# Unnormalised probabilities, gates scaled by turned reciprocals, dense sums for A's norms, half-size high parts and a new order in a hybrid attention trunk

## The reference, cut to what matters

```python
for layer in range(2):
    proj = rms_norm(h, norm_pre[layer]) @ w_in[layer]       # split over the branches
    A: q = rms_norm(c_q, q_norm) @ w_uq                     # c_q has 192 columns
       kv = rms_norm(c_kv, kv_norm) @ w_ukv                 # c_kv has 128 columns
       p = softmax(mask(q @ k^T * scale)); o = p @ v
    B: three dilated patterns merged by their denominators  # here one softmax with a bias
    C: top 128 keys of an indexer, softmax over them, p @ v
    D: a = softmax(s0) - lam * softmax(s1); o = rms_norm(a @ v)
    y = concat(A, B, C, D) * silu(gate) @ w_out[layer]
    h = h + rms_norm(y, norm_post[layer])
```

## Time and profile before

| | |
|---|---|
| median of three runs | 716.22 us (714.87 to 717.11) |
| the profiled execution | 717.92 us |
| its span, first to last instruction | 716.1 us |
| mean granted clock of PE | 0.976 of full |
| PE busy | 676.5 us (94%) |
| DVE, ACT, POOL busy | 432.3, 330.3, 242.1 us |
| DMA | 80.96 MB, 113 GB/s on the mean |

### The profile page before, as it was taken

The page is one execution under the profiler, slowest core; times in us unless marked ns, Lnnn a source line. Parts: engine busy times, 40 slices in busy tenths (PEclk is TensorE's granted clock), DMA queues, the critical chain, the costliest instruction groups (busy, mean ns, idle before and its releaser), DMA issues. The chain is left out here.

```text
span 716.1 us, 10494 instructions
## 1 busy us (share of the span) xinstructions
PE 676.5 (94%) x3840; PEld 545.0 (76%) x3840; DVE 432.3 (60%) x1068; ACT 330.3 (46%) x751; POOL 242.1 (34%) x209
## 2 busy tenths in 40 slices
PE   6999999999999998799999999999999999978996
PEld 4888887887897754369998897788889776445896
DVE  4313897899797554640470269888978865456114
ACT  5424535653434637742353264465533354666121
POOL 1432633335055612002424536125323663200030
PEclk9999999999999969999999999999999997899999
DMA  8458876332322101112363598442322221030202
GB/s 249 131 176 244 231 215 237 95 107 67 111 85 85 59 1 58 60 27 95 118 177 110 178 257 230 123 132 74 105 75 74 79 70 59 0 118 1 90 28 91
DMA packets 66644, 80.96 MB, mean 113 GB/s; under 512 B 10737, under 2 KB 52337, under 8 KB 66593
## 3 DMA queue, kind: packets, MB, share of 16 engines
q1 hardware_dynamic: 66593, 80.29, 36.6%
HBM read 69.76 MB, written 13.93 MB: 117 GB/s over the span
## 5 line engine op out<-in xcount | busy, mean ns | idle before, releaser
L652 POOL TENSOR_TENSOR w_low<-w_raw,w_high 128x512 fp32r<-128x512 f32 (+2 forms) x156 | 199.2, 1309 | 383.2 <-ACT w_high L692 383.2
L1184 PE MATMUL bank<-uT,w_high 128*128 128x512 f32 x400 | 160.0, 400 | 0.2 <-DVE staging L998 0.2
L1186 PE MATMUL bank<-uT,w_low 128*128 128x512 f32 x400 | 158.3, 396 | 0.0
L1185 PE MATMUL bank<-uT,w_high 128*128 128x512 f32 x400 | 158.1, 395 | 0.0
L800 ACT ACTIVATE probs<-probs,negmax 128x128 f32<-128x128 f32 (+3 forms) x160 | 89.1, 559 | 95.7 <-DVE negmax L1039 95.4
L1184 PEld LDWEIGHTS bank<-uT,w_high 128*128 128x128 f32 x400 | 75.5, 189 | 18.6 <-issue 1.3
L1186 PEld LDWEIGHTS bank<-uT,w_low 128*128 128x128 f32 x400 | 75.4, 189 | 17.8
L1185 PEld LDWEIGHTS bank<-uT,w_high 128*128 128x128 f32 x400 | 75.5, 189 | 16.2
L692 ACT ACTIVATE w_high<-w_raw 128x2048 fp32r<-128x2048 f32 (+2 forms) x39 | 72.7, 1865 | 26.1 <-DMA w_raw<-in_w_out 23.1
L1184 PE MATMUL bank<-w_high,mix 128*128 128x256 f32 x256 | 72.4, 283 | 1.0 <-DVE mix L1124 1.0
L1186 PE MATMUL bank<-w_high,mix 128*128 128x256 f32 x256 | 71.6, 280 | 0.0
(11 more groups left out here) (150 smaller groups left out, 1089.4 us busy)
## 6 DMA issues: line engine op xcount, KB each, us to landing
w_raw<-in_w_in SPq DMA_DIRECT2D x27, 1024.0 KB, 5.4
w_raw<-in_w_out SPq DMA_DIRECT2D x8, 1024.0 KB, 4.9
parts_dram<-staging SPq DMA_DIRECT2D x12, 512.0 KB, 4.9
strips<-strips_dram SPq DMA_DIRECT2D x24, 256.0 KB, 4.4
dqk<-parts_dram SPq DMA_DIRECT2D x24, 256.0 KB, 4.4
hX<-in_x SPq DMA_DIRECT2D x8, 512.0 KB, 6.0
qidx<-parts_dram SPq DMA_DIRECT2D x12, 256.0 KB, 4.2
w_raw<-in_w_in SPq DMA_DIRECT2D x4, 512.0 KB, 5.4
```

The source lines that it names most:

```text
L652: ins = nc.gpsimd.tensor_tensor(w_low[:, s, ks, 0:w], w_raw[:, s, ks, 0:w], w_high[:, s, ks, 0:w].bitcast(F32), ALU.subtract)
L1184: nc.tensor.matmul(out_ap, lh, rh, start=start, stop=False)
L1185: nc.tensor.matmul(out_ap, lh, rl, start=False, stop=False)
L1186: return nc.tensor.matmul(out_ap, ll, rh, start=False, stop=stop)
```

## The change

1. `norm j` for B, C and A leaves the probabilities as they are and takes only the reciprocal. Their `turn` no longer waits for DVE, but block by block for the exponential.
2. A new step `wide i` (ACT) spreads the reciprocals of a pair of heads over 64 columns each, `spread i` transposes that on PE into a work bank (four transposes) and DVE multiplies the gate by it, one 128x512 operation. There are six pairs in each layer. `pv` waits for it.
3. `asums` replaces the twelve narrow matmuls by three with 64 columns of ones as weights and 512 columns moving; ACT copies the bank out, SP stores two rows of it to DRAM and `aload` loads them with the tokens on the partitions. It stands among the units of B's values, `squares_a` three steps earlier, in a room of its own.
4. `high` writes two halves of 128x1024, and POOL starts on the first.
5. `SCHEDULE` is another order in nearly all of its lines.

```diff
                 else:
-                    after(nc.vector.reciprocal(inv[:, i, 0], sums[:, i, 0]))
-                    for q in range(NB):
-                        sl = slice(POFF[q], POFF[q] + WID[q])
-                        ins = nc.vector.tensor_scalar(probs[bufs[0]][:, sl], probs[bufs[0]][:, sl],
-                                                      inv[:, i, 0, q:q + 1], None, ALU.mult)
-                ins.then_inc(probs_ready, 1)
+                    nc.vector.reciprocal(inv[:, i, 0], sums[:, i, 0]).then_inc(inv_ready, 1)
...
                     if kb == 0:
-                        pe.wait_ge(probs_ready, jj + 1)
+                        if JOBS[j][0] == "D":
+                            pe.wait_ge(probs_ready, l * HEADS + j + 1)
...
                     for q in range(kb, NB):
+                        if kb == 0 and JOBS[j][0] != "D":
+                            pe.wait_ge(exp_done, l * NSJ + S_AT[j] + q + 1)
...
+                if kind == "wide":
+                    i = step[1]
+                    j = PV_JOBS[i][0]
+                    act.wait_ge(inv_ready, l * (NJ - HEADS) + j - HEADS + 2)
...
+                    nc.scalar.activation(wide[i % 2][:].rearrange("p q h d -> p h q d"),
+                                         inv[:, j % 4:j % 4 + 2, 0, :].unsqueeze(3).to_broadcast([P, 2, NB, HD]),
+                                         ACT.Copy).then_inc(wide_ready, 1)
...
+                if kind == "spread":
+                    n = l * NU + UNIT_AT[step]
+                    pe.wait_ge(wide_ready, l * NWIDE + step[1] - HEADS + 1)
+                    b = work_bank(n)
+                    for q in range(NB):
+                        ins = nc.tensor.transpose(b[:, q * P:(q + 1) * P],
+                                                  wide[step[1] % 2][:, q].rearrange("p h d -> p (h d)"), ident[:])
...
+                if kind == "spread":
...
+                    nc.vector.tensor_tensor(gate[:, k, :], bank[:, unit_bank(n), :], gate[:, k, :], ALU.mult
+                                            ).then_inc(emptied_by["dve"], 1)
...
-                if kind == "aup_head":
+                if kind == "asums":
                     n = l * NU + UNIT_AT[step]
                     pe.wait_ge(lat_squared, l + 1)
                     b = work_bank(n)
...
+                    nc.tensor.matmul(b[0:HD, :], ones[:], sq[:, 0, :], start=True, stop=False)
+                    nc.tensor.matmul(b[HD:P, :], ones[:], sq[:, 2, :], start=True, stop=True)
+                    nc.tensor.matmul(b[0:HD, :], ones[0:QL - P, :], sq[0:QL - P, 1, :], start=False, stop=True
+                                     ).then_inc(unit_ready, 1)
...
+                for half in range(2):
+                    ks = slice(4 * half, 4 * half + 4)
+                    nc.scalar.activation(w_high[:, g % SLOTS, ks, 0:w], w_raw[:, g % SLOTS, ks, 0:w], ACT.Copy
+                                         ).then_inc(w_high_done, 1)
...
-    scores 13 0 2, norm 12, scores 13 2 4, pv 7, mix 3, mix 2, turn 12 0, turn 12 1, turn 12 2, turn 12 3
+    scores 13 0 2, spread 7, turn 11 2, turn 11 3, scores 13 2 4, norm 12, mix 3, pv 7, mix 2, turn 12 0, turn 12 1, turn 12 2, norm 13, turn 12 3, turn 13 0
```

More of the change, by code:

```diff
@@ L112 @@
[L112 to L119, removed]
@@ L125 @@
-    scores 15 0 2, norm 14, scores 15 2 4, pv 8, mix 5, turn 14 0, turn 14 1, turn 14 2, turn 14 3, norm 15, ya 0, turn 15 0, turn 15 1, ya 2, turn 15 2, turn 15 3, ya 1, pv 9, mix 0, mix 1
+    unit cq 0, unit cq 1, unit qi 0, unit qi 1, unit dq 0, idx 0, unit dq 1, idx 1, unit dv 0, idx 2, unit dv 1, idx 3, unit dv 2, idx 4, unit dv 3, idx 5, unit dk 0, idx 6, idx 7, topk 1, unit dk 1, topk 3, unit gd 0
+    scores 0 0 2, topk 4, unit gd 1, scores 0 2 5, topk 2, unit gb 0, scores 0 5 7, scores 0 7 8, norm 0, unit gb 1, turn 0 0
@@ new lines @@
+    scores 5 0 2, turn 3 3, topk 1, unit ck 0, turn 4 0, norm 4, turn 4 1, topk 1, scores 5 2 4, topk 1, turn 4 2, turn 4 3, topk 1, pv 3, topk 1, topk 1, topk 1, unit ck 1, topk 1
+    scores 6 0 1, unit bv 0, topk 1, unit bv 1, unit bv 2, norm 5, dsquares 1, scores 6 1 4, dscale 1, topk 1, turn 5 0, turn 5 1, asums, topk 1, topk 2, unit bv 3, topk 1, topk 1, topk 1, wide 4, dnorm 1
+    scores 7 0 3, topk 1, topk 2, turn 5 2, fill 8, norm 6, turn 5 3, topk 1, unit gc 0, fill 9, topk 3, scores 7 3 4, unit gc 1, norm 7, turn 6 0, fill 10, spread 4, fill 11, pv 4, turn 6 1, turn 6 2
@@ new lines @@
+    scores 8 0 2, turn 6 3, turn 7 0, scores 8 2 4, wide 5, turn 7 1, unit ga 0, aload, turn 7 2, turn 7 3, spread 5, pv 5
+    scores 9 0 1, turn 8 0, turn 8 1, norm 8, aup_head, unit ga 1, mix 6, turn 8 2, scores 9 1 4, aup 0, turn 8 3, aup 1, turn 9 0, norm 9
+    scores 10 0 1, turn 9 1, aturn 0, wide 6, scores 10 1 4, aup 2
+    scores 11 0 1, turn 9 2, scores 11 1 4, norm 10, spread 6, turn 9 3, aturn 1, pv 6, aup 3, turn 10 0, aturn 2, turn 10 1, turn 10 2, mix 7, norm 11, turn 10 3, aturn 3, turn 11 0, turn 11 1, wide 7
@@ L126 @@
+    scores 12 0 2, scores 12 2 4
+    scores 13 0 2, spread 7, turn 11 2, turn 11 3, scores 13 2 4, norm 12, mix 3, pv 7, mix 2, turn 12 0, turn 12 1, turn 12 2, norm 13, turn 12 3, turn 13 0
+    scores 14 0 2, turn 13 1, wide 8, turn 13 2, scores 14 2 4
+    scores 15 0 1, norm 14, mix 4, mix 5, turn 13 3, scores 15 1 4, spread 8, norm 15, turn 14 0, pv 8, ya 0, wide 9, turn 14 1, turn 14 2, turn 14 3, turn 15 0, turn 15 1, spread 9, turn 15 2, turn 15 3, ya 2, pv 9, mix 0, mix 1, ya 1
 """
@@ L373, in trunk @@
         lampr = at("lampr", "Y", [P, DEPTH, 2, DQK], F32, skip=10 * KB)
+        wide = [at(f"wide{i}", "wide", [P, NB, 2, HD], F32, skip=2 * KB * i) for i in range(2)]
         tiny_at = [arena["small"]]
@@ L1055, in _ @@
                     else:
-                        k = 2 * "ABC".index(br) + h // 2
+                        k = gate_of(step[1])
+                        wait_unit_emptied(dve, l * NU + UNIT_AT[("spread", step[1])])
                         nc.vector.scalar_tensor_tensor(gate[:, k, :], bank[:, PV, :], 0.5, gate[:, k, :],
@@ L1388, in _ @@
                 if kind == "ya":
-                    wait_unit_emptied(pe, l * NU + NU - 1)
+                    if step[1] == 0:
+                        wait_unit_emptied(pe, max(n for n in range(l * NU, (l + 1) * NU) if unit_bank(n) == WORK))
                     pe.wait_ge(shifted, (l + 1) * NSJ)
```

94 lines of the change are left out of this document (64 added, 30 removed).

## The result

The changed kernel takes 691.42 us (median of four runs, 689.43 to 692.30) against 716.66 us for four runs of the kernel before: a ratio of 0.963, 95% interval 0.959 to 0.966, 25 us less. The forecast was 701, its range 690 to 714: right in direction and within the range, but the gain is 25 us where 15.5 were worked out. It lies outside the forecast's own 694 to 708, at the 691 of the rival that PE's gaps go as a whole, to which the prediction gave 0.12.

A forecast was written before the change was run, and what follows sets the result against it. PE's own stream was taken to bound the kernel, with PE busy 676.5 of 716.1 us. Terms -11 (clock), -3.2 (sums), +6.7 (spreads), -8 (waits) sum to -15.5, giving 701 us; 8-in-10 range 690 to 714.

The forecast's parts named there:

- PE's gaps go as a whole: Rival: all 2.5 and 5.9 us idle before and in A's heads go, clock's whole 12.5 won; 691 us, chance 0.12.
- The clock: Up-projection between C's and A's heads: 13.6 us a layer at half speed return to full clock; -11 us, between 0 and -12.5.
- D's scores: New order in D: the 1.22 us wait and its clock loss go, new waits arise; 0, between -5 and +5.
- The rival on transposes: Clock keeps falling near the up-projection, as if transposes don't count as PE-busy like matmuls; 712 us, chance 0.14.
- The sums: A's latents: three dense fp32 products, 1.9 us, replace 3.5 us of narrow matmuls a layer; -3.2 us in all.
- The spreads: Six a layer for B, C and A, 48 transposes at 0.14 us, all paid by PE; +6.7 us.
- The waits: Unnormalised probabilities cut PE's idle time in A's heads by 3.5 and before them by 0.5 us a layer; -8 in all.
- The cap for A's heads: A's heads, a 26 us stretch: with ACT at 20.5 us of work, not less than 23.5 us expected.
- the slower rival: DVE's queue holds D's scores, clock follows: 724 us, chance 0.12; sign: over 5 us of PE waiting for negmax.

## Why the prediction was right, and where its sizes were off

*What bounds the kernel.* PE's stream, at 94% and now 96%. Right: DVE lost 38 us of work, ACT gained 8, and neither shows but by what PE waited for.

*The clock.* The forecast took -11 and kept the fall in D's scores for another term. All three falls are gone, 30.8 us, which by the ratio of 0.54 is 14 us. The account has two halves. The narrow sums bring the clock down: shown, since putting them alone into the changed kernel brought two falls, and taking them out of the old order left the first layer's up-projection at full speed. That they do so because a single column moves, as the prediction suggests, is not shown; 64 columns did so too. And the absence of other falls is no gift of the sums: the dense sums alone left 20.4 us at half speed, two of three falls in places where the kernel before had none.

*The rival on transposes.* The Trainium skill (TensorE: Matmul & The Clock Gate, on transposes) says that transposes don't count as PE-busy in the way that matmuls do. The traces don't bear out a fall by it here: with 48 transposes more in the stream, and with 96 more (spreads doubled), the granted clock stayed at 1.00 up to 688 us. No run takes transposes by themselves. The rival's time would have been 712.

*The sums.* -3.2 forecast, two times 3.5 less 2.0 us measured, -3.0.

*The spreads.* This term was mis-sized: +6.7 forecast, 2.4 us measured by leaving them out and 2.5 by doubling them. The price of one transpose, 0.14, was the 0.98 us of a row of seven, which takes in the tail of the last one; from start to start it is 0.11. And I let PE pay for all of it though it had idle time beside 4 of the 12.

*The waits.* -8 forecast for A's heads and the up-projection, 12 measured: 8.4 us of idle time a layer became 2.3 and 2.5. The cause that I gave was wrong. I had put the 1.43 us in the earlier trace rows and the like down to the four scaling operations in DVE's queue; without them, in the old order, the same wait is 1.43 us and the total for ACT's copies 8.3. It is the parting of scores and turns that takes these waits away: 6.2 us by the run with A's heads in the old order, 6.1 by its reverse. The unscaled probabilities are what this order needs, as the run with scaled ones shows. I had also left 2.0 of the 2.5 us before A's heads standing; the order ahead of them took 1.2 away, with the waits for ACT's values and aqk. The cap for A's heads, ACT's 20.5 us of work and so not under 23.5, was a guess, and worked out unevenly: 23.5 less PE's 21.8 leaves 1.7 us idle, so 4.2 of the 5.9 would have gone, where I counted 3.5. ACT did 20.80 us in 25.3, in step with a PE at 96%; what was capped wrongly is PE's idle time.

*D's scores.* 0 forecast. The wait of 1.22 us, which the kernel before has in both layers, and its fall in the second are gone; the new one stands where it was expected, at the second job's fourth score, with 0.51 us and not 1, and without a fall. All waits for a shift are 1.4 us, far from the 5 that would have been the sign of the slower rival. This term came out better than even by the 1.7 us of the clock.

Together: -14 for the clock, -3.0, +5.1 for the spreads in busy time, -15.0 of idle time are -26.9, against -26.2 of the span. In spans the forecast's error is 10.7 us. With the spreads at 5.1 us of work less the 2.9 of idle time that they fill, it is made of 3.0 for the clock, 4.5 for the spreads and 4.1 for the waits, less 0.2 for the sums and 0.7 that the terms don't explain. The three large ones are all on one side. So the range held by its width, not by the sum: the time is that of the rival "gaps as a whole", and that by other terms, since the rival had 16.8 us of waits and spreads at their full price.

A ladder of medians, each kernel with its batch's own kernel before as 1: dense sums 0.990, with unscaled probabilities 0.981, with A's heads in the new order 0.973, all of the order 0.963. Read the other way round the steps have other sizes: unscaled probabilities are worth nothing beside narrow sums and the old order, and some 60 us in the new one.

What stays open: why the clock fell at one wait and not at another of the same length. The second pass of the up-projection waited 1.72 us in both layers of the run with dense sums alone and fell in one, and the kernel before waited 1.22 us among D's scores in both layers and fell in one.

## What to carry to other kernels

A change of dependencies and a change of order belong together: the first without the second was worth nothing beside narrow sums (0.997) and 5 to 6 us beside dense ones, the second without the first cost some 60 us. When PE is the bound, look for the stretches in which it is busy at the lower clock, and at what stands just before them; here matmuls of one column counted as busy in the profile throughout and still brought the clock down. Put what a wait needs far ahead of it: four steps in other places cost 26 us, 10 of it as idle time and 16 as longer work, behind waits at half speed. And before a wait is put down to an operation, take the operation out and keep the order: here the wait stayed.

## What the hardware showed that was not expected

With the narrow sums put back, eleven of the 24 dense matmuls behind them still ran at the lower clock in the first layer (6.8 us at half speed with PE busy for 6.76), and in the second layer the clock fell only when three dense matmuls had run at the upper one. Twelve fp32 products with 64 moving columns did not hold the clock either: it fell to 0.50 with the last of them, for 10.2 us in both layers. And two fp32 products over the two halves of the columns started 0.01 us apart and took 1.0 us together (206.05 to 207.06), the time of the third one alone (207.06 to 208.06).
